# Finding the keys of sixteen best pairs on GpSimd in place of VectorE, with indices and gates one batch later

## The reference, cut to what matters

```python
s1 = einsum('thd,hkd->thk', q1, sub_keys_1)      # 128 scores a head and side
v1, i1 = lax.top_k(s1, 16); v2, i2 = lax.top_k(s2, 16)
cand = v1[..., :, None] + v2[..., None, :]        # 16 x 16 sums of pairs
top_s, top_pos = lax.top_k(cand.reshape(t, 8, 256), 16)
expert_idx = take_along_axis(i1[..., :, None] * 128 + i2[..., None, :], top_pos)
gates = softmax(top_s)
a = einsum('thkd,td->thk', expert_u[expert_idx], xb)
out = einsum('thk,thkd->td', gelu(a) * gates, expert_v[expert_idx])
```

## Time and profile before

| what | value |
|---|---|
| time, median of 3 runs | 2957.23 us (2957.08 to 2959.57) |
| the profiled execution's own time | 2961.6 us |
| its span, first to last instruction | 2959.4 us |
| mean granted TensorE clock | 0.949 |
| busy, share of the span: PE, DVE, ACT, POOL | 93%, 64%, 44%, 22% |
| GpSimd: 256 gathers of u, 256 of v | 297.4 us and 311.5 us busy |
| VectorE: 512 half dots | 304.0 us and 302.7 us for two records of 256 |

### The profile page before, as it was taken

The page is one execution under the profiler, slowest core; times in us unless marked ns, Lnnn a source line. Parts: engine busy times, 40 slices in busy tenths (PEclk is TensorE's granted clock), DMA queues, the critical chain, the costliest instruction groups (busy, mean ns, idle before and its releaser), DMA issues.

```text
span 2959.4 us, 47035 instructions
## 1 busy us (share of the span) xinstructions
PE 2748.9 (93%) x18175; PEld 2078.1 (70%) x18175; DVE 1881.6 (64%) x3067; ACT 1296.6 (44%) x2473; POOL 663.6 (22%) x576
## 2 busy tenths in 40 slices
PE   8999899999999998999999999999998878888885
PEld 8996788888888887989999889677764432222221
DVE  7885566565565565455445558888858874555556
ACT  5555443333333344435334345555566532233223
POOL 0000000000000000040000002444447675555554
PEclk9999999999999998999999999999996679999997
DMA  6443545555555553443555656999999999999998
GB/s 257 176 166 127 199 174 189 192 184 185 189 193 184 186 190 124 157 147 141 183 185 184 241 199 243 372 408 417 412 385 411 405 407 423 422 422 419 419 419 347
DMA packets 132598, 790.37 MB, mean 267 GB/s; under 512 B 34774, under 2 KB 34774, under 8 KB 37142
## 3 DMA queue, kind: packets, MB, share of 16 engines
q1 hardware_dynamic: 55040, 393.16, 35.9%
q0 software_dynamic: 77008, 394.46, 33.0%
q10 hardware_dynamic: 384, 0.52, 0.1%
HBM read 944.95 MB, written 4.19 MB: 321 GB/s over the span
## 4 chain that ended last, share of the span: by engine, by line
PE 65%; DMA 17%; DVE 10%; issue 4%; ACT 2%; POOL 2%; POOLq 0%; DVEq 0%; ACTq 0%
PE bank L2073 12%; PE bank L2074 12%; PE bank L2075 12%; DMA s_u<-in_expert_u,s_u_index 11%; PE bank L2079 10%; PE bank L2515 5%; DMA s_v<-in_expert_v,s_v_index 5%; PE bank L2080 5%; DVE s_u L1933 3%; PE bank L2570 3%; PE bank L2525 2%; DVE s_w_lo L1306 1%; POOL s_u L658 1%; DVE s_yrow L1614 1%; PE bank L2171 1%
## 5 line engine op out<-in xcount | busy, mean ns | idle before, releaser
L1306 DVE TENSOR_TENSOR s_w_lo<-s_raw,s_w_hi 128x2048 fp32r<-128x2048 f32 x288 | 661.3, 2296 | 597.0 <-ACT s_w_hi L705 592.9
L705 ACT ACTIVATE s_w_hi<-s_raw 128x2048 fp32r<-128x2048 f32 x284 | 543.9, 1915 | 805.6 <-PE bank L2075 530.0
L2079 PE MATMUL bank<-s_a,s_w_hi 128*128 128x512 f32 x1408 | 495.0, 394 | 3.2 <-DVE s_w_lo L1306 3.2
L2073 PE MATMUL bank<-s_a,s_w_hi 128*128 128x256 f32 (+1 forms) x1632 | 465.5, 285 | 3.4 <-DVE s_a L1330 1.8
L2075 PE MATMUL bank<-s_a,s_w_lo 128*128 128x256 f32 (+1 forms) x1632 | 463.1, 284 | 0.0
L2074 PE MATMUL bank<-s_a,s_w_hi 128*128 128x256 f32 (+1 forms) x1632 | 462.7, 284 | 0.0
L1933 DVE CUSTOM_DVE_ANT_0 s_u<-s_u,s_xn_late 128x1024 f32<-128x1024 f32 x256 | 304.0, 1225 | 223.7 <-DMA s_u<-in_expert_u,s_u_index 197.3
L2570 PE MATMUL bank<-s_v,s_spread 128*32 128x512 f32 x2048 | 309.0, 715 | 139.3 <-DMA s_v<-in_expert_v,s_v_index 107.0
L2080 PE MATMUL bank<-s_a,s_w_lo 128*128 128x256 f32 x1408 | 395.3, 281 | 0.0
L658 POOL DMA_INDIRECT s_u<-in_expert_u,s_u_index x256 | 297.4, 1162 | 359.9 <-DVE s_halfdot L1933 207.3
L678 POOL DMA_INDIRECT s_v<-in_expert_v,s_v_index x256 | 311.5, 1217 | 231.0 <-PE bank L2570 140.3
(11 more groups left out here) (352 smaller groups left out, 3397.4 us busy)
## 6 DMA issues: line engine op xcount, KB each, us to landing
s_raw<-in_stream SPq DMA_DIRECT2D x292, 1024.0 KB, 4.8
s_raw<-in_expert_v SPq DMA_DIRECT2D x40, 1024.0 KB
s_raw<-in_dense_u SPq DMA_DIRECT2D x37, 1024.0 KB
s_tap_blocks<-in_taps POOLq DMA_DIRECT2D x9, 512.0 KB, 3.5
s_u<-in_expert_u,s_u_index POOLq DMA_INDIRECT x256
s_v<-in_expert_v,s_v_index POOLq DMA_INDIRECT x256
s_panel_early<-in_dense_u POOLq DMA_DIRECT2D x3, 1024.0 KB, 10.8
s_xres<-in_x SPq DMA_DIRECT2D x2, 1024.0 KB, 6.0
```

The costliest lines, as they stand in the source:

```text
L705: act.activation(w_hi[s % 2][:, :], raw[s][:, :], ACT.Copy).then_inc(hi_ready, 1)
L1306: dve.tensor_tensor(w_lo[s % 2][:, :], raw[s][:, :], w_hi[s % 2][:, :].bitcast(f32), ALU.subtract)\
L2073: pe.matmul(dst, left[0], right[0], start=start, stop=False)
L2079: pe.matmul(dst, left[0], both, start=start, stop=False)
```

## The change

VectorE's three instructions of 128x512 (L1895, L1897, L1900) go for the 13 routes 3 to 15. In turn 2, right after `best_pairs`, VectorE now makes row and column (the two shifts) and raises `pos_ready`. GpSimd copies these and the key numbers, compares (a subtraction and a test for zero, since it keeps to two instructions), multiplies, and adds up 16 numbers in four halving steps, nine instructions in all, and raises `pairs_picked`. It does so in its loop at k = 4 (b + 2) for the route of batch b, after `gather_u(k)` and `gather_v(k - 4)`. VectorE waits for `pairs_picked` in turn 2 of batch b + 1, then makes the indices (`experts_of`) and the gates. ScalarE's `v_indices` follows one batch later as well. The key numbers `ind` get a second buffer, and the new GpSimd tiles lie in memory that `s_one_key_more` uses from batch 17 on. Routes 0 to 2 keep the old way.

```diff
@@ gpsimd
+            def pairs_picked_of(th):
+                both = pool_pick[:, :].rearrange("p (s a) -> p s a", a=TOPK)
+                halves = pool_pick[:, :].rearrange("p (h k a) -> p h k a", h=2, a=TOPK)
+                pool.wait_ge(pos_ready, th - EARLY + 1)
+                step(pool.tensor_copy(pool_ind[:, :], ind[th % 2][:, :]))
+                link(pool.tensor_copy(pool_pos[:, :], pos_of[:, :]))
+                link(pool.tensor_tensor(both, iota_f[:, 0:TOPK].unsqueeze(1).to_broadcast([128, 2 * TOPK, TOPK]),
+                                        pool_pos[:, :].unsqueeze(2).to_broadcast([128, 2 * TOPK, TOPK]), ALU.subtract))
+                link(pool.tensor_scalar(both, both, 0.0, None, ALU.is_equal))
+                link(pool.tensor_tensor(halves, halves, pool_ind[:, :].rearrange("p (h a) -> p h a", h=2).unsqueeze(2).to_broadcast([128, 2, TOPK, TOPK]),
+                                        ALU.mult))
+                for width in (8, 4, 2):
+                    link(pool.tensor_tensor(both[:, :, 0:width], both[:, :, 0:width], both[:, :, width:2 * width], ALU.add))
+                keys_of = picked[th // PH][:, 0:2 * SLOTS].rearrange("p (h s) -> p h s", h=2)[:, :, th % PH * TOPK:(th % PH + 1) * TOPK]
+                pool.tensor_tensor(keys_of, halves[:, :, :, 0], halves[:, :, :, 1], ALU.add).then_inc(pairs_picked, 1)
...
                 if k >= LAG + NV:
                     gather_v(k - LAG)
+                if k % BATCH == 0 and k >= 2 * BATCH and route_in(k // BATCH - 2):
+                    pairs_picked_of(route_in(k // BATCH - 2))
@@ scalar
                         gate_exps(route_in(g - 1))
-                        v_indices(route_in(g - 1))
+                    if g > 1 and route_in(g - 2):
+                        v_indices(route_in(g - 2))
@@ vector, route(th, turn)
                 elif turn == 2:
                     best_pairs()
-                else:
-                    pairs_experts(th)
+                    step(dve.tensor_scalar(pos_of[:, 0:TOPK], pos[:, :], 4, None, ALU.logical_shift_right))
+                    dve.tensor_scalar(pos_of[:, TOPK:], pos[:, :], TOPK - 1, None, ALU.bitwise_and).then_inc(pos_ready, 1)
@@ vector, loop over g and turn
                     if turn == 2 and g and route_in(g - 1):
+                        dve.wait_ge(pairs_picked, route_in(g - 1) - EARLY + 1)
+                        experts_of(route_in(g - 1))
                         gates_softmax(route_in(g - 1))
```

More of the change, by code:

```diff
@@ L403, in two_layers @@
     one_key = place("s_one_key", [128, 16 * NKEYS], S + 16 * K)
-    one_key_more = small("s_one_key_more", 8 * NKEYS)
+    more_at = spot(8 * NKEYS)
+    one_key_more = place("s_one_key_more", [128, 8 * NKEYS], more_at)
+    pool_pick = place("s_pool_pick", [128, 2 * TOPK * TOPK], more_at)
+    pool_pos = place("s_pool_pos", [128, 2 * TOPK], more_at + 8 * TOPK * TOPK + 128)
+    pool_ind = place("s_pool_ind", [128, 2 * TOPK], more_at + 8 * TOPK * TOPK + 256)
     pick_at = spot(2 * TOPK * TOPK)
@@ L413, in two_layers @@
     val = small("s_val", 2 * TOPK)
-    ind = small("s_ind", 2 * TOPK, u32)
+    ind = [small("s_ind0", 2 * TOPK, u32), place("s_ind1", [128, 2 * TOPK], more_at + 8 * TOPK * TOPK, u32)]
     top = small("s_top", TOPK)
@@ L488, in two_layers @@
         expert_ready, v_index_ready = sem("expert_ready"), sem("v_index_ready")
+        pos_ready, pairs_picked = sem("pos_ready"), sem("pairs_picked")
         gate_max, gate_exp = sem("gate_max"), sem("gate_exp")
@@ L1878, in best_keys @@
                 part = slice(half * TOPK, (half + 1) * TOPK)
-                sixteen(val[:, part], ind[:, part], score[:, score_row(th), keys_of], sc_rest[:, :])
+                sixteen(val[:, part], ind[th % 2][:, part], score[:, score_row(th), keys_of], sc_rest[:, :])
             def best_pairs():
@@ L1887, in best_pairs, with pairs_located, pairs_experts @@
                 dve.tensor_scalar(gsum[:, 0:1], top[:, 0:1], -1.0, None, ALU.mult).then_inc(gate_max, 1)
-            def pairs_experts(th):
+            def pairs_located():
                 step(dve.tensor_scalar(pos_of[:, 0:TOPK], pos[:, :], 4, None, ALU.logical_shift_right))
                 link(dve.tensor_scalar(pos_of[:, TOPK:], pos[:, :], TOPK - 1, None, ALU.bitwise_and))
+            def pairs_experts(th):
+                pairs_located()
                 both = pick[:, :].rearrange("p (s a) -> p s a", a=TOPK)
@@ L1896, in pairs_experts @@
                                        pos_of[:, :].unsqueeze(2).to_broadcast([128, 2 * TOPK, TOPK]), ALU.is_equal))
-                link(dve.tensor_tensor(halves, halves, ind[:, :].rearrange("p (h a) -> p h a", h=2).unsqueeze(2).to_broadcast([128, 2, TOPK, TOPK]),
+                link(dve.tensor_tensor(halves, halves, ind[th % 2][:, :].rearrange("p (h a) -> p h a", h=2).unsqueeze(2).to_broadcast([128, 2, TOPK, TOPK]),
                                        ALU.mult))
@@ L1900, in pairs_experts, with experts_of @@
                 link(dve.tensor_reduce(keys_of, halves, AX.X, ALU.add))
+                experts_of(th)
+            def experts_of(th):
+                keys_of = picked[th // PH][:, 0:2 * SLOTS].rearrange("p (h s) -> p h s", h=2)[:, :, th % PH * TOPK:(th % PH + 1) * TOPK]
                 wait(dve, v_index_ready, th - 1)
```

## The result

The changed kernel takes 2964.22 us (median of 20 runs, 2960.45 to 2968.25); the kernel before, on the same chips, 2959.02 us (20 runs). The ratio is 1.0019, interval [1.0012, 1.0025], so about 5.2 us more: slower, and just inside the 0.2% that was called no change, which the interval's upper end (0.25%) exceeds. The forecast of 2958.5 us is 5.7 us low. The wide range of 2948 to 2975 holds the time; the forecast's own range, 2952 to 2964, misses it by 0.2 us. The profiled executions have spans of 2964.3 and 2959.4 us.

The account below looks back on a forecast made before the run. VectorE was taken to bound the kernel until 1970 us, then TensorE, with DMA nearly full. Gain -2.0 and loss +3.3 sum to +1.3 on 2961.6, 2962.9; median 4.4 lower: 2958.5 us, own range 2952 to 2964, wide range 2948 to 2975.

Parts of the forecast that it names:

- What bounds, and the cap: Batches 1 to 16: VectorE leads by a hair until 1970, then TensorE; DMA has only 2.0 us to give from 1861.
- The relief: VectorE, freed of 2.16 us a batch, keeps 1.16; capped by DMA's room, this gains 2.0 us in all.
- X: GpSimd's time for the nine look-up instructions of one route: taken as 9.1 us, ends 6.4 and 17.4.
- What VectorE pays: VectorE's half dots start late behind GpSimd instructions at the shared ports: 1.0 us a batch, ends zero and 6.4.
- The rival that paid 4 us a batch: Ports cost VectorE 4 us, so 22.4 us a batch against 20.1; 2968.7 us in all; chance 0.08.
- Gathers of v and indices one batch late: Routes 3 to 15 are first gathered in batch 12 or later, so the delay costs nothing in itself.
- The wait for `pairs_picked`: VectorE in turn 2 has 11.2 us for picks of 9.1, so no wait; one for one from X = 11.
- Does GpSimd have the time?: GpSimd has 8.5 us a batch beside gathers; picks overdraw 0.6, 8 in all; batches 7 and 14 return 17.
- it decides from X = 9.8 on: Rival GpSimd pace: lag over the stage is 13 (X - 8.5) - 17, 15.5 us at X = 11; chance 0.16.
- The loss: DMA may run dry in six pauses of batches 3 to 8, 0.55 us each, 3.3 us in all.
- The signs: Trace marks set beforehand; right: batches of about 19.5 us before 1970; wrong: nine instructions above 11 us, step 17 after 2190.
- GpSimd becomes the pace: Rival: GpSimd's gathers plus picks set batch time, slower; 2972.7 us at X = 11; chance 0.16.

Follow-up runs that it names:

- e1: Changed kernel without the look-up: VectorE copies best keys instead of GpSimd's nine instructions, so other experts are gathered; 2934.7 us, 0.992 of the kernel before.
- e6: Changed kernel, but GpSimd's nine instructions fill an unread tile, and VectorE waits for them, then does its own three; 2973.59 us, 1.0055 of the kernel before.
- e2: Changed kernel with the look-up back on VectorE, indices and gates still one batch later; 2957.65 us, 0.9997 of the kernel before.
- e4: Changed kernel with the comparison on VectorE; GpSimd keeps the key-number copy, product and additions; 2958.56 us, 1.0001 of the kernel before.
- e8: Changed kernel with GpSimd's subtraction made three times per route; 2986.55 us, 1.0095 of the kernel before.
- e9: Changed kernel with only route 3 picked on GpSimd, the twelve others on VectorE one batch later; 2960.68 us, 1.0006 of the kernel before.
- e3: Changed kernel with GpSimd's nine instructions split into three parts behind successive gather pairs; 2962.66 us, 1.0017 of the kernel before.
- e10: Changed kernel with routes 4 to 15 picked on GpSimd and route 3 on VectorE; 2964.64 us, 1.0021 of the kernel before.
- e7: Changed kernel with only odd routes picked on GpSimd, even ones on VectorE one batch later; 2962.67 us, 1.0016 of the kernel before.
- e5: As e1, but first keys repeated so that as many rows are gathered as before; 2978.0 us, 1.0068 of the kernel before.

## Why the prediction was right, and where it was not

- **What bounds, and the cap.** "Time is won only where DMA still has room" agrees with the ledger, whose bytes give the spans. But the prediction read the room from DMA's busy share, and that step doesn't hold: at shares of 0.99 to 1.01 the kernel before moved 396 to 406 GB/s between 1886 and 1986 us, and the relieved one (e1) 421 to 424. The relief was taken at -2.0 us; alone it is worth 1.4 to 2.5 us by the gathers and 5 by the bytes, and beside the load some 10 (e6).
- **The nine instructions.** X = 9.1 us; the thirteen in the trace take 7.3 to 10.2, mean 9.0. Right; the lower end of 6.4 was not reached by a whole block.
- **What VectorE pays.** 1.0 us a batch; half dots of 1310 ns in place of 1222, 142 times over 13 routes, are 0.96. The half dot from 1914.24 took 2.28 us: the product on GpSimd had begun at 1913.89 and ended at 1915.45, and the dot ended 1.07 us later, where an undisturbed half takes 1.22. So it was held for about as long as the product ran. That agrees, within 0.15 us, with the exclusive lock of the Trainium skill, SBUF — State Buffer, section on SBUF's two separate sides. The rival that paid 4 us a batch falls by the 0.96; it had also set its 22.4 us against the stage's mean of 20.1 and not against VectorE's 20.58.
- **Gathers of v and indices one batch late:** nothing, right (e2).
- **The wait for `pairs_picked`.** "So nothing" failed: VectorE waits 18.1 us in eleven waits, the longest 3.2. For batch 4 the step had VectorE asking at 1918.7; it asked at 1916.54, since it was relieved, and the picks ended at 1918.33, since gather 16 of v went out at 1907.68 and not 1906.48. A relieved engine comes earlier to the wait.
- **Does GpSimd have the time?** This step failed: "13 x 0.6 = 8 is less than 17, so the buffers carry it", and with it the rival's "it decides from X = 9.8 on". It decided at 9.0. The batch that fits these runs is not the stage's mean of 20.1 us but what VectorE could do without its look-up: 18.65 us (e1), about 19.6 with held dots. Less 11.2 of gathers and 0.55 that leaves 6.9 to 7.9 us, a bound that is worked out and that no run between 5.4 and 9.0 tested. 5.4 us (e4) fit, 9.0 don't, and 11.9 (e8) cost much more. After the pick that batch 7 spares, GpSimd waited 10.3 us for VectorE (four waits between 1998 and 2030), so the time "given back" was not all used, and the changed kernel made up none of its bytes there (2.50 MB behind by 1986, 2.55 by 2036). They can be made up: e9 regained its 1.4 MB by 1961, when no further pick came.
- **The loss.** 0.55 us for each of six pauses, 3.3 in all, is the term that was mis-sized most: the load without the relief costs 15.1 us (e6). By 2111 the changed kernel lies 4.65 MB, 11 us, behind; about half comes back from 2161 on, mostly because the profiled execution of the kernel before loses 1.8 MB there itself. That return wasn't foreseen either.
- **The sum.** -2.0 and +3.3 stand against about -10 and +15. The two errors largely cancel, so that the total came within 5.7 us and stayed at 0.2% is luck and not the mechanism.
- **The signs.** Of the right signs, batches of about 19.5 us, an early DMA share of 0.9 or above and VectorE without waits above 1 us did not come: 21.4 us a batch, 0.78 in the window from 1861, and waits of up to 3.2. The wrong signs came true in part: GpSimd was without idle time from 1865 to 1998 and from 2030 to 2148; DMA was below 0.85 in one window; step 17 on TensorE came at 2188.19, within the bound of 2190.

So it was the rival "GpSimd becomes the pace", at a third of its price, that came true. Up to 1970 that is shown (e3, e4, e8, e10). From 1986 to 2111 the changed kernel loses 2.1 MB more. There, too, GpSimd hardly waits from 2030 on, and gathers 44 to 64 of u go out at 21.3 us a batch, against 20.9 in the kernel before and 23.3 in e8, so the same pace is likely. But kernels without picks there lose some of it as well (e9 1.3 MB, e2 0.55). Why e7, which leaves GpSimd time, loses 2.5 MB in that stretch stays open: its trace shows VectorE late with a buffer just ahead of a pick, and no experiment took this apart.

## What to carry to other kernels

An engine that issues the transfers isn't idle while it waits for a buffer: compare its new work with the batch that the relieved engine would reach, not with the batch of today. Add up bytes by windows against the kernel before; where DMA is full at the end, the bytes missing give the time lost, and show where. Don't read the room that DMA has left from its busy share alone; look at GB/s as well. Relief of the engine in front also makes that engine come earlier to every new wait.

## What the runs showed of the hardware

- A DMA share near 1.00 went with different rates while gathers of the same rows went out: 396 to 406 GB/s from 1886 to 1986 us in the kernel before, 421 to 424 in e1. Why was not tried.
- The same bytes in as many packets took longer when other rows were gathered: 403 in place of 420 GB/s at a full DMA share (e5). Why was not tried.
- On GpSimd a test against a constant on 128x512 took 1.50 us undisturbed, longer than the subtraction of two tiles of that size, 1.05 us; a copy of 32 numbers took 0.21 us undisturbed and up to 1.26 us held.
